# A decoder layer with product-key experts: query projection by token halves, first selections behind their chunk, low parts between pieces of routing

## Time and profile before

| what | us |
|---|---|
| median of three runs | 1987.07 |
| the profiled execution, its own time | 1997.52 |
| its span | 1995.7 |
| PE busy | 1633.1 (82%) |
| DVE busy | 1381.3 (69%) |
| POOL busy | 544.4 (27%) |
| ACT busy | 322.7 (16%) |
| mean granted clock of PE, as a share of 2.4 GHz | 0.898 |

### The profile page before, as it was taken

The page is one execution under the profiler, slowest core; times in us unless marked ns, Lnnn a source line. Parts: engine busy times, 40 slices in busy tenths (PEclk is TensorE's granted clock), DMA queues, the critical chain, the costliest instruction groups (busy, mean ns, idle before and its releaser), DMA issues.

```text
span 1995.7 us, 18994 instructions
## 1 busy us (share of the span) xinstructions
PE 1633.1 (82%) x6668; PEld 1191.1 (60%) x6668; DVE 1381.3 (69%) x2790; ACT 322.7 (16%) x658; POOL 544.4 (27%) x516
## 2 busy tenths in 40 slices
PE   2798999989997999999999967789999899980000
PEld 1686877767776788888888866654444344430000
DVE  5656456666554268899888579985555566679998
ACT  2242244436413221111111100000000000000001
POOL 0000000000000003353444420014444544457773
PEclk7899999989998999999999986669999899995555
DMA  7323311132423228999998960019999999999995
GB/s 292 140 92 147 127 64 64 64 127 106 169 95 106 74 72 311 356 365 375 353 369 322 386 253 0 1 52 392 376 374 375 412 409 409 410 409 388 367 384 230
DMA packets 123070, 489.76 MB, mean 245 GB/s; under 512 B 13792, under 2 KB 14048, under 8 KB 113632
## 3 DMA queue, kind: packets, MB, share of 16 engines
q0 software_dynamic: 73728, 268.47, 35.2%
q1 hardware_dynamic: 49248, 220.09, 29.3%
HBM read 483.78 MB, written 4.72 MB: 245 GB/s over the span
## 4 chain that ended last, share of the span: by engine, by line
DVE 37%; DMA 30%; PE 22%; issue 3%; DVEq 3%; ACT 2%; POOL 2%; SPq 0%; ACTq 0%; POOLq 0%
DMA ring<-in_down,idx 18%; DMA ring<-in_up,idx 10%; DVE accum L1428 10%; PE bank L449 6%; PE bank L450 6%; PE bank L451 6%; DVE ring L1269 6%; DVE h2T L1398 3%; DVE h2T L1397 2%; DVE wmat L1408 2%; POOL ring L1453 2%; DVE acc_ada L956 1%; DMA raw<-in_ada 1%; DVE onehot L1352 1%; PE bank L535 1%
## 5 line engine op out<-in xcount | busy, mean ns | idle before, releaser
L1453 POOL DMA_INDIRECT ring<-in_down,idx x256 | 278.8, 1089 | 1249.8 <-DVE idx L1360 759.7
L700 PE MATMUL bank<-stream,wmat 128*128 128x512 f32 x1024 | 444.2, 597 | 9.1 <-DMA stream<-in_up 8.3
L678 PE MATMUL bank<-h2T,stream 128*128 128x256 f32 x2048 | 444.3, 380 | 2.6 <-ACT wmat L930 2.6
L1269 DVE CUSTOM_DVE_ANT_0 ring<-ring,h2row 128x1024 f32<-128x1024 f32 x256 | 311.6, 1222 | 167.2 <-DMA ring<-in_down,idx 164.1
L678 PEld LDWEIGHTS bank<-h2T,stream 128*128 128x128 f32 x2048 | 390.1, 191 | 56.2 <-issue 3.0
L1428 DVE SCALAR_TENSOR_TENSOR accum<-ring,share,accum 128x1024 f32<-128x1024 f32 x256 | 328.8, 1284 | 107.6 <-DMA ring<-in_up,idx 94.1
L700 PEld LDWEIGHTS bank<-stream,wmat 128*128 128x128 f32 x1024 | 196.0, 192 | 256.7 <-issue 246.5
L1453 POOL DMA_INDIRECT ring<-in_up,idx x256 | 265.4, 1037 | 172.5 <-DVE accum L1428 119.2
L449 PE MATMUL bank<-hT_hi,whi 128*128 128x512 f32 x384 | 160.9, 419 | 23.5 <-DVE hT_lo L1006 17.0
L975 DVE TENSOR_TENSOR wlo<-raw,whi 128x2048 fp32r<-128x2048 f32 x45 | 103.0, 2290 | 108.4 <-ACT whi L722 108.0
L690 PE MATMUL bank<-h2T 128*128 128x128 f32 x512 | 114.1, 393 | 49.9 <-DVE h2T L1398 49.9
(11 more groups left out here) (201 smaller groups left out, 1596.8 us busy)
## 6 DMA issues: line engine op xcount, KB each, us to landing
stream<-in_downT SPq DMA_DIRECT2D x128, 512.0 KB, 6.5
stream<-in_up SPq DMA_DIRECT2D x128, 512.0 KB, 6.8
raw<-in_ada SPq DMA_DIRECT2D x24, 1024.0 KB, 6.0
raw<-in_w_query SPq DMA_DIRECT2D x8, 1024.0 KB, 4.9
raw<-in_w_xp SPq DMA_DIRECT2D x4, 1024.0 KB, 6.0
raw<-in_w_gateA SPq DMA_DIRECT2D x4, 1024.0 KB, 4.9
raw<-in_w_branchP SPq DMA_DIRECT2D x4, 1024.0 KB, 4.8
raw<-in_w_q SPq DMA_DIRECT2D x4, 1024.0 KB, 4.8
```

The costliest lines, as they stand in the source:

```text
L678: last = pe.matmul(bank[:, 4 + i % 2, 0:DT], stream[:, i % RING, k * P:(k + 1) * P], h2T[:, k, GB * P:S], start=(k == 0), stop=(k == KT - 1))
L700: last = pe.matmul(bank[:, 2 * tb + half, :], wmat[:, wslot(i), tb * P:(tb + 1) * P], stream[:, (ET + i) % RING, half * S:(half + 1) * S], ...
L1269: dve.tensor_tensor_reduce(out=ring[g % RING][:, :], in0=ring[g % RING][:, :], in1=h2row[:, b, :], scale=1.0, scalar=0.0, op0=ALU.mult, op ...
L1453: pool.indirect_dma_start(out=ring[slot][:, :], out_offset=None, in_=table, in_offset=bass.IndirectOffsetOnAxis(ap=idx[:, b, k:k + 1], axi ...
```

## The change

Parts of it:

- The query stage becomes two, `queryA` (tokens 0 to 255) and `queryB` (tokens 256 to 511), of eight half chunks each; every weight chunk of the query is read, split and used twice.
- The norm behind the out stage is done by halves too (`norm2(half)` on DVE, `shifted(half)` on ACT, which now also adds the shift to h2T itself). The high and low parts are written to hT_hi and hT_lo instead of r1.
- A score tile holds one head for 256 tokens; it is computed behind the next chunk.
- DVE does the first selection of each head (`stage1(half, c)`, four rows) behind the low parts of chunk c+2 in half A. The second selection and what follows is `stage2(n)`. In `stage2(0)` the low parts of half B are put in between, one for each 4.0 us of routing work by a table of costs. Then come `stage2(1)`, `stage1(1, 0..7)`, `stage2(2)`, `stage2(3)`, with one dot for each 1.4 us of routing work.
- `match_replace` works in place. DOTS_FIRST goes from 40 to 64.
- The gate row is made in the out stage, at chunk 1. The transposes of x1 are in two parts, before out chunk 3 and before chunk 1 of queryA. Both stores to memory are issued behind the load of chunk 4 of queryA. POOL waits for x1's store instead of the gate row's.
- ACT's waits for routing are now one, on `routes_done` at tile 88 of the downT stream. wmat is no longer rotated by SLOT0.

The places of EXP_AT and PICK_AT, `softmax`, `dots` and what follows the routing stay.

```diff
-DOTS_FIRST = 40
+DOTS_FIRST = 64
+ROUTE_PER_WLO = 4.0
+ROUTE_PER_DOT = 1.4
...
+        if (s, c) == ("out", 3):
+            tiles += [("x1tok", 2 * n, "act") for n in range(4)]
+        if (s, c) == ("queryA", 1):
+            tiles += [("x1tok", 2 * n + 1, "act") for n in range(4)]
+        if (s, c) == ("queryA", 3):
             tiles += [("h2tok", n, "act") for n in range(2 * GB)]
...
+        if s in HALF and (s, c) != ("queryA", 0):
+            tiles.append(("score",) + score_before(s, c) + ("act",))
+    tiles.append(("score", 15, "act"))
...
+            sp.wait_ge(ahi_ready, N_OP["norm2"] + 2 * KT)
             for n in range(2 * ET):
                 if n >= RING:
                     sp.wait_ge(tile_used, n - RING + 1)
                 src = downT[n] if n < ET else up[(n - ET) * P:(n - ET + 1) * P, :]
                 sp.dma_start(stream[:, n % RING, :], src).then_inc(stream_in[n % RING], 16)
+                if n == 2:
+                    wait_emptied(sp, "score", 15)
...
+            def shifted(half):
+
+                toks = slice(half * HT, (half + 1) * HT)
+                for k in range(KT):
+                    act.wait_ge(part_ready, 24 + half * KT + k + 1)
+                    act.activation(hT_hi[:, k, toks], h2T[:, k, toks], ACT.Identity, bias=modc[:, 24 + k:25 + k])
+                    act.activation(h2T[:, k, toks], h2T[:, k, toks], ACT.Identity,
+                                   bias=modc[:, 24 + k:25 + k]).then_inc(ahi_ready, 1)
...
+                elif stage == "out" and c == 3:
+                    for k in range(0, 8, 2):
+                        x1_out(k)
+                    root(N_MEAN["norm2"], 1.0 / D)
+                    shifted(0)
+                elif stage in HALF:
+                    if (stage, c) == ("queryA", 1):
+                        shifted(1)
+                        for k in range(1, 8, 2):
+                            x1_out(k)
...
-                if 70 <= i < 70 + 8 * TB and i % 8 == 6:
-                    act.wait_ge(logit_ready, (i - 70) // 8 + 1)
-                if i == 102:
-                    act.wait_ge(pick_ready, DB)
+                if i == 88:
+                    act.wait_ge(routes_done, 1)
                 act.wait_ge(tile_used, i + 1)
...
+            def fill_lows(us):
+
+                split[1] += us
+                if split[1] >= ROUTE_PER_WLO and split[0] < len(CHUNKS):
+                    follow(split[0])
+                    split[0] += 1
+                    split[1] = 0.0
+
+            def fill(us):
+
+                credit[0] += us
+                while credit[0] >= ROUTE_PER_DOT:
+                    credit[0] -= ROUTE_PER_DOT
+                    dots(1, P)
...
+            def stage1(half, c, fill):
+
+                wait_emptied(dve, "score", 8 * half + c)
+                rows_ = [(tb, m) for tb in range(2) for m in range(2)]
+                top16([top_v[:, tb, c, m] for tb, m in rows_], [top_i[:, tb, c, m] for tb, m in rows_],
+                      [s_all[:, c, tb, m] for tb, m in rows_], fill)
+                dve.sem_inc(s1_done, 1)
...
-            for n in range(TB):
-                for g in range(4):
-                    wait_emptied(dve, "score", 4 * n + g)
-                route(n, 1 if n else 0)
+            for c in range(PH):
+                if c < 7:
+                    follow(split[0])
+                    split[0] += 1
+                stage1(0, c, nothing)
+            stage2(0, fill_lows)
+            while split[0] < len(CHUNKS):
+                follow(split[0])
+                split[0] += 1
+            stage2(1, fill)
+            for c in range(PH):
+                stage1(1, c, fill)
+            for n in range(GB, TB):
+                stage2(n, fill)
+            dve.sem_inc(routes_done, 1)
             for b in range(DB):
                 softmax(GB + b).then_inc(pick_ready, 1)
```

More of the change, by code:

```diff
@@ L100, in slot_of, with score_before @@
     return WOVEN + (g + 12) // 4, (g + 12) % 4
+def score_before(s, c):
+    return (8 * HALF[s] + c - 1,)
 def tile_plan():
@@ L107, in tile_plan @@
     for s, c in CHUNKS:
-        if (s, c) == ("query", 0):
-            tiles += [("x1tok", n, "act") for n in range(8)]
-        if (s, c) == ("query", 4):
+        if (s, c) == ("out", 1):
+            tiles += [("gaterow", n, "dve") for n in range(2)]
+        if (s, c) == ("out", 3):
[3 more added lines that the diff above has]
+        if (s, c) == ("queryA", 3):
             tiles += [("h2tok", n, "act") for n in range(2 * GB)]
-            tiles += [("gaterow", n, "dve") for n in range(2)]
         if s == "pool":
@@ L581, in tokens_first, with score @@
                 return t
+            def score(t, u):
+                c = u % 8
+                free_bank(t)
+                if u == 0:
+                    pe.wait_ge(pos_in, 48)
+                wait_emptied(pe, "queryB" if u >= 8 else "queryA", 2 * c + 1)
+                for tb in range(2):
+                    for m in range(2):
+                        last = pe.matmul(bank[:, BANK[t], (2 * tb + m) * P:(2 * tb + m + 1) * P],
+                                         q2T[:, c % 2, m, tb * P:(tb + 1) * P], subk[:, m, :],
+                                         start=True, stop=True)
+                last.then_inc(tile_ready, 1)
+                return t + 1
             t = 0
@@ L589, in _ @@
                         o_columns(h)
[L590 to L595, removed]
+                if (stage, c) == ("out", 1):
                     for m in range(2):
                         free_bank(t)
+                        if m == 0:
+                            pe.wait_ge(ada_acc, 6)
                         pe.matmul(bank[:, BANK[t], :], ones[:, :], acc_ada[:, 1, m * S:(m + 1) * S],
@@ L600, in _ @@
                         t += 1
+                if (stage, c) == ("out", 3):
+                    wait_emptied(pe, "out", 3)
+                    t = tokens_first(t, x1T, range(0, 8, 2))
+                if (stage, c) == ("queryA", 0):
+                    norm2_mean()
+                if (stage, c) == ("queryA", 1):
+                    t = tokens_first(t, x1T, range(1, 8, 2))
+                if (stage, c) == ("queryA", 3):
+                    pe.wait_ge(ahi_ready, N_OP["norm2"] + KT)
+                    t = tokens_first(t, h2T, range(2 * GB))
                 if c == 0:
                     ready = {"xp": "norm1", "pool": "pooled", "branchP": "ya",
-                             "out": "merged", "query": "norm2"}.get(stage)
+                             "out": "merged"}.get(stage)
                     if ready:
@@ L639, in _ @@
                                 pe.wait_ge(alo_ready, N_OP["o"] + k + 1)
-                            last = mm3(bank[:, BANK[t], :], wh[:, k, m * P:(m + 1) * P],
-                                       wl[:, k, m * P:(m + 1) * P], ah[:, k, :], al[:, k, :],
+                            toks = slice(0, S)
+                            if stage in HALF:
+                                toks = slice(HALF[stage] * HT, (HALF[stage] + 1) * HT)
+                                if c == 0 and m == 0:
+                                    pe.wait_ge(alo_ready, N_OP["norm2"] + HALF[stage] * KT + k + 1)
+                            last = mm3(bank[:, BANK[t], 0:toks.stop - toks.start], wh[:, k, m * P:(m + 1) * P],
+                                       wl[:, k, m * P:(m + 1) * P], ah[:, k, toks], al[:, k, toks],
                                        k == 0, k == KT - 1)
@@ L644, in _ @@
                         t += 1
[L646 to L657, removed]
+                    if stage in HALF and (stage, c) != ("queryA", 0):
+                        t = score(t, *score_before(stage, c))
+            t = score(t, 15)
             def stream_tile(n):
@@ L699, in _ @@
                     for half in range(2):
-                        last = pe.matmul(bank[:, 2 * tb + half, :], wmat[:, wslot(i), tb * P:(tb + 1) * P],
+                        last = pe.matmul(bank[:, 2 * tb + half, :], wmat[:, i, tb * P:(tb + 1) * P],
                                          stream[:, (ET + i) % RING, half * S:(half + 1) * S],
@@ L884, in _ @@
                         act.activation(hT_hi[:, i, :], tmpo[:, i, :], ACT.Copy).then_inc(ahi_ready, 1)
[L885 to L896, removed]
+                elif stage == "out" and c == 3:
[4 more added lines that the diff above has]
+                elif stage in HALF:
+                    if (stage, c) == ("queryA", 1):
+                        shifted(1)
+                        for k in range(1, 8, 2):
+                            x1_out(k)
+                    if (stage, c) == ("queryA", 3):
                         for k in range(2 * GB):
+                            if k == 0:
+                                act.wait_ge(part_ready, 24 + 2 * KT)
                             act.activation(h2row[:, k // 2, (k % 2) * S:(k % 2 + 1) * S],
@@ L900, in _ @@
                     for m in range(2):
```

(32 more changed lines are left out.)

158 lines of the change are left out of this document (93 added, 65 removed).

## The result

The changed kernel takes 2094.29 us (median of four runs, 2089.74 to 2096.37), the kernel before 1988.39 beside it: a ratio of 1.0535, 95% interval 1.0507 to 1.0563. The profiled execution has a span of 2087.9 us for 1995.7. The forecast was 2074, in a range of 2040 to 2108.

A forecast was written before the change was run, and what follows sets the result against it. It took three dates to bound the kernel: first gather, stream start, first one-hot. One-hots 122.5 us later less 36 in the tail gave +87: 2084 in profile, 2074 as median, range 2040 to 2108.

The forecast's parts named there:

- Out stage and start of the halves: Out stage to chunk A1: reciprocal ends at 603.9, A1 starts at 624.4 after a new 9 us PE wait.
- The query: Half chunks on PE: 5.75 us each, 12 us idle before B1, stream starts 30.7 us later, idx 22.4 us earlier.
- The hold: Before softmax: routing ends at about 988 with 89 dots, then DVE waits 112 us for ACT's exponentials at tile 100.
- Dots behind the hold: After softmax: 103 dots remain, 60 without a stream taking 103 us; first one-hot at 1300, 122.5 us later.
- 1.71 each, which I take: Price in us of a dot without the stream beside it, between bounds of 1.36 and 2.29.
- the landing time of five gathers: Gathered rows just behind the stream land in 5.4 us, 7.7 beside it; used to price a dot without stream.
- The tail: After the one-hots: 64 dots for 88, more accumulations left behind the up stream; gain 36 us, bounds 33 and 55.
- The sum: Whole kernel: +122.5 us at the first one-hot less 36 in the tail, +87 us.
- My step from 2084 to 2074: From profiled execution to median: the median of the runs before was 10 us under its profiled execution.
- the end follows the first gather: Rival on the gather ring and DVE: the whole line of gathers moves 22 us ahead, 1965; chance 0.05.
- hold and gain are both absent: Rival: no hold of DVE, later stream and fewer routing dots stay; dots end 38 later, less 36, 1989; chance 0.03.
- The granted clock: Rival on PE in the query: pauses at half A's chunks keep the clock at 1.2 GHz, 2120; chance 0.06.

The follow-up runs named there:

- e1: Changed kernel with ACT's exponentials at tile 68 of the downT stream instead of 100, nothing else; 1999.83 us, 1.0073 of before.
- e2: Changed kernel with ACT's exponentials at tile 84 instead of 100; 2049.61 us, 1.0319 of before.
- e8: Kernel before with only a hold: exponentials at tile 124, picks at 126, ACT waiting at tile 102 for routing's end; 2051.40 us, 1.0305 of before.
- e7: Changed kernel with ACT's odd x1 tile copies before its second-half activations and B1's low parts before the eighth first selection; 2086.68 us, 1.0479.
- e4: Kernel before with DOTS_FIRST 64 instead of 40, nothing else; 1995.86 us, 1.0065 of before.
- e3: Changed kernel with exponentials at tile 68 instead of 100 and DOTS_FIRST 40 instead of 64; 2005.60 us, 1.0106 of before.
- e10: Changed kernel with EXP_AT 79, ROUTE_PER_DOT 1.1, DOTS_FIRST 54, odd x1 tile copies and B1's low parts ordered earlier; 1983.62 us, 0.9969 of before.

## Why the prediction was right

**Out stage and start of the halves: right.** The reciprocal ended at 603.7 for 603.9. ACT's sixteen activations are 0.40 apart, PE waits 7.5 us for the copy of the odd tile (9 forecast) and goes on at 624.8 (624.4 forecast).

**The query: right at its end, with two small errors that cancel.** A half chunk takes 6.64 - 0.90 = 5.74 us for 5.75. PE waits 12.7 us for B1 (12 forecast), whose low parts are done at 702.5 and not at 700.2; in return a half chunk with scores takes 6.64 for 6.85. The stream starts at 752.9 for 752.3, idx is done at 738.9 for 736.8. The Trainium skill's figure of N/2.4 + 2.5 ns (TensorE: Matmul & The Clock Gate, Back-to-back issue gap), which is for a single matmul, is not reached here either: 48 matmuls in 5.74 us are 119.6 ns, not 109, as the rows of before said.

**The hold: right.** Routing ended at 987 for 988, with 89 dots, and DVE waited 113.8 us for 112. This is the step that decides; e1, e2 and e8 show it from three sides. Of the 94 us by which routing ends earlier (1081 before), some 45 are no gain at all: 37 dots of 1.22 us were moved out of it, and they have to be done behind it.

**Dots behind the hold: the size was off.** The step "1.71 each, which I take" is the term that was mis-sized. Dots without a stream cost 1.87 us (61 in 114 us), 1.87 in e2, 1.89 in e7 and 1.93 in e8. With about 60 of them that is the 10 us by which the one-hots came later than 1300. I had taken the landing time of five gathers just behind the stream, 5.4 us, and it was right, 5.5 for 55 gathers. What the chain shows besides is POOL: dots come in bursts, their gathers are issued one behind the other, 1.8 us for the first, and two or three of them stand in the chain ahead of a landing, where my price had left less room: 6.86 us for four dots less 5.4 of landing is 1.46, and measured it is 7.48 less 5.5, 1.98. That POOL makes this difference was not tested:

```profile
1246.22 1.78 POOL ring L1558
1248.00 0.30 issue
1248.30 1.18 POOL ring L1558
1249.48 0.30 issue
1249.79 1.57 POOL ring L1558
1251.36 0.30 issue
1251.66 6.01 DMA ring<-in_down,idx
```

**The tail: right.** 41 was saved in the profile for 36 forecast. In the profiles of the seven kernels with 64 dots the stretch from the start of the last one-hot to the end takes 622.6 to 627.7 us, in the four with 40 dots 656.6 to 665.2, and the means are 35 apart. The profile of before has the longest of them, 665.2, so the 41 is 5 or 6 too much, and 36 was a good price.

**The sum.** In spans, +92.2 for +86.5: +133.2 at the one-hots less 41. In medians it is +105.9. The rest is that the profiled execution of before lies 9 us over its median and that of the changed kernel 5 under its own. My step from 2084 to 2074 lays the change of the spans on the medians, and there the change is 13.7 us larger. 5 or 6 of these are the long tail in the profile of before; with a tail worth 35 the one-hots' 133.2 make +98, 11 over my +87, 10 of which are the price of a dot alone. The other 8 us no step and no run explains.

**The rivals.** That the end follows the first gather fell: idx came 20 us earlier and DVE could not use it. That hold and gain are both absent is what e1 shows, nearly: I priced it at 1989, 2 us over before, and e1 is 2000, 14 over its own before; e4's 10 us for the raised DOTS_FIRST would be a part of that, which no run separates. The granted clock stayed at 1.00 over the short pauses between the chunks of half A and fell in the two long ones (window, length, busy, clock, DMA share, GB/s; 0.50 is the lower level, and a stretch that holds both shows a value between):

```profile
625.00:630.00 5.00, 5.00 (x27) 0.58 0.62 262
...
680.00:685.00 5.00, 3.85 (x33) 1.00 0.18 33
...
700.00:705.00 5.00, 2.43 (x11) 0.50 0.27 69
705.00:710.00 5.00, 5.00 (x34) 0.73 0.43 157
```

The Trainium skill (TensorE: Matmul & The Clock Gate, HAM oscillation) warns of waits behind each tile that return every tile to the low clock. The pauses of 7.5 and 12.7 us did end at the low clock here, those of 1.1 to 1.5 did not; the waits of the page's example are longer than these short ones, so this doesn't contradict it.

## What to carry to other kernels

When work is moved earlier on one engine, look for places on other engines that are fixed by a count and hand something back to it. Here the exponentials sat at tile 100, 12 us ahead of where routing used to end; routing ended 94 us earlier and the constant stayed, so the gain turned into a wait of the same size, and a change of one number gave nearly all of it back. And a shorter first stretch is worth little if it is only made of what another engine will wait for: with the hold gone, the whole reordering stands between +1.1% (e3) and -0.3% (e10), by how well three constants and two small orders are fitted to each other.

## What was not expected

Gathers of 512 KB through a ring of four don't fill the DMA engines even when they are alone: 286 GB/s and a share of 0.83, 1.87 us each, while the accumulations through a ring of eight run at 1.36 us and 378 GB/s. Beside the stream the same ring gives 2.2 us a dot. So taking the stream away, some 40% of the bytes (512 KB each 3.45 us, 152 of 368 GB/s), makes a dot only a sixth faster. Whether a longer ring would help was not tried.
